# RWKV scan: the eight diagonal blocks of a lane in one transfer from evenly spaced DRAM rows, 8 loads a chunk in place of 16

## The reference, cut to what matters

```python
def step(S, inp):
    r_t, w_t, k_t, v_t, kk_t, b_t = inp
    sa = jnp.einsum('bhij,bhj->bhi', S, -kk_t)
    S = (S * w_t[:, :, None, :] + sa[..., None] * b_t[:, :, None, :]
         + v_t[..., None] * k_t[:, :, None, :])
    return S, jnp.einsum('bhij,bhj->bhi', S, r_t)
```

## Time and profile before

| | us |
|---|---|
| Median of 3 runs | 3494.68 |
| Lowest and highest of them | 3493.44, 3499.32 |
| The profiled execution | 3487.46 |
| Its span, first to last instruction | 3486.2 |

### The profile page before, as it was taken

How to read it: one execution, slowest core, us unless ns; L and a number is a source line. 1 busy time by engine, 2 the same in 40 slices (tenths; PEclk the granted TensorE clock), 3 DMA queues, 4 the chain that set the end, 5 groups by cost and what they waited for, 6 DMA issues and landing times.

```text
span 3486.2 us, 58522 instructions
## 1 busy us (share of the span) xinstructions
PE 3188.2 (91%) x25755; PEld 2622.4 (75%) x25755; DVE 2211.3 (63%) x2948; ACT 971.9 (28%) x1514; POOL 469.5 (13%) x373
## 2 busy tenths in 40 slices
PE   6988788979987999999999897998998799999996
PEld 4777767778885878888888676875667688888885
DVE  5758655778887444444444575997556566666666
ACT  4544233312113221111111444112663111111112
POOL 2530023423224000000000121000001011111110
PEclk9979788989998999999999998999999899999999
DMA  4410044322224011111111202114001111111111
GB/s 131 122 66 14 16 142 138 111 45 42 37 36 166 19 55 51 40 55 53 38 55 43 91 31 74 49 43 99 2 2 61 43 49 49 49 49 49 49 49 67
DMA packets 242726, 207.27 MB, mean 59 GB/s; under 512 B 66744, under 2 KB 205255, under 8 KB 241959
## 3 DMA queue, kind: packets, MB, share of 16 engines
q1 hardware_dynamic: 223527, 176.82, 17.1%
q10 hardware_dynamic: 13824, 25.17, 2.2%
q0 software_dynamic: 5120, 1.53, 0.5%
HBM read 171.93 MB, written 29.64 MB: 58 GB/s over the span
## 4 chain that ended last, share of the span: by engine, by line
PE 70%; DVE 17%; ACT 5%; POOL 2%; issue 2%; DMA 2%; SPq 1%; ACTq 0%; DVEq 0%; POOLq 0%
PE ps L2169 23%; PE ps L2184 17%; PE ps L2031 5%; PE ps L636 3%; PE ps L637 3%; PE ps L638 3%; DVE Yc L2794 2%; DVE s_tmp L1662 2%; DVE s_Z L1663 2%; PE ps L2893 2%; PE ps L2921 1%; PE ps L2911 1%; PE ps L1480 1%; POOL a_x L2544 1%; PE ps L1008 1%
## 5 line engine op out<-in xcount | busy, mean ns | idle before, releaser
L3198 DVE TENSOR_TENSOR H<-H,ps 128x1024 f32<-128x1024 f32 x256 | 312.7, 1221 | 181.6 <-PE ps L2184 174.8
L2334 DVE TENSOR_TENSOR fsum<-fsum,ps 128x1024 f32<-128x1024 f32 x168 | 205.2, 1221 | 312.4 <-PE ps L2184 310.3
L2184 PE MATMUL ps<-dh,hh 128*128 128x512 f32 x864 | 340.0, 393 | 19.9 <-DVE hl L2149 13.9
L2184 PE MATMUL ps<-dl,hh 128*128 128x512 f32 x864 | 338.7, 392 | 0.0
L2184 PE MATMUL ps<-dh,hl 128*128 128x512 f32 x864 | 338.6, 392 | 0.0
L2169 PE MATMUL ps<-hn_h,uh 128*128 128x512 f32 x704 | 275.8, 392 | 7.2 <-DVE ul L1779 4.7
L2169 PE MATMUL ps<-hn_l,uh 128*128 128x512 f32 x704 | 275.4, 391 | 0.0
L2169 PE MATMUL ps<-hn_h,ul 128*128 128x512 f32 x704 | 275.3, 391 | 0.0
L2169 PE MATMUL ps<-hx_h,uh 128*128 128x512 f32 x512 | 200.9, 392 | 8.4 <-DVE hx_l L2149 5.3
L2184 PEld LDWEIGHTS ps<-dh,hh 128*128 128x128 f32 x864 | 163.8, 190 | 58.0 <-DVE hl L2149 15.6
L2169 PE MATMUL ps<-hx_l,uh 128*128 128x512 f32 x512 | 200.4, 391 | 0.0
(11 more groups left out here) (473 smaller groups left out, 7345.8 us busy)
## 6 DMA issues: line engine op xcount, KB each, us to landing
aw<-in_w_ada_dram ACTq DMA_DIRECT2D x96, 256.0 KB, 2.9
uw<-in_w_mlp_dram SPq DMA_DIRECT2D x32, 512.0 KB, 4.3
dw<-in_w_mlp_dram SPq DMA_DIRECT2D x32, 512.0 KB, 5.2
uw<-in_ffn_gate_dram SPq DMA_DIRECT2D x22, 512.0 KB, 4.0
uw<-in_ffn_up_dram SPq DMA_DIRECT2D x22, 512.0 KB, 5.3
dw<-in_ffn_down_dram SPq DMA_DIRECT2D x22, 512.0 KB, 5.9
cw<-in_w_in_dram SPq DMA_DIRECT2D x20, 512.0 KB, 3.8
o_w<-in_w_out_dram SPq DMA_DIRECT2D x16, 512.0 KB, 9.9
```

The lines of the kernel that those rows point to most:

```text
L2184: mm = pe.e.matmul(ps[:, 2 * pair + hf, :], v[s][:, blk(t)], w[:, half(hf)], start=(m == 0), stop=(m == 2))
L2334: return dve.c.tensor_tensor(f, f, new, ALU.add) if g else dve.c.tensor_copy(f, new)
L3198: return dve.c.tensor_tensor(h, h, self.ps[:, 4 + 2 * (t % 2):6 + 2 * (t % 2), :], ALU.add)
```

## The change

The scratch `nd` gets another shape: for each lane two halves (one for each head of the pair) of 64x64 elements and 64 elements of padding. With the padding, going from one diagonal block to the next is always 16 rows and 16 columns, 1,040 elements, also from the last block of the first half to the first block of the second. So one load can take the 8 blocks of a lane: 8 by 16 rows by 64 bytes. There are 8 loads, of 8 KB each, SP has 4 of them (x = 0 and 1), POOL the other 4.

Three things follow. The store of `NM` is made in two DMAs, one for each half of the partitions, both ahead of the `ZZ` loads in SP's queue. The order of the partitions of `N16` and `Z16` becomes x, k in place of k, x. And the store of `Z16` to `zd`, whose DRAM order stays k, x, so writes its 32 rows of 4 KB as 4 groups (x) of 8 (k), the rows of a group 16 KB apart; it was one contiguous run.

```diff
-                         ("nd", (2, LANES, PART, CH)), ...
+                         ("nd", (2, LANES, 2, CH * CH + CH)), ...
-    def blocks_there(self, eng, counter, n, ks):
-        nd = self.dram["nd"]
-        for k in ks:
+    def blocks_there(self, eng, counter, n, xs):
+        nd = self.dram["nd"][n % 2]
+        for x in xs:
             for d in range(2):
-                eng.e.dma_start(self.N16[4 * k:4 * k + 4, d], nd[n % 2, 4 * d:4 * d + 4, 16 * k:16 * k + 16, 16 * (k % 4):16 * (k % 4) + 16]) \
+                eng.e.dma_start(self.N16[8 * x:8 * x + 8, d], bass.AP(tensor=nd.tensor, offset=nd[4 * d + x].offset, ap=[[16 * CH + 16, 8], [CH, 16], [1, 16]])) \
                     .then_inc(*counter.one("in", n))
...
-            sp.e.dma_start(nd[n % 2].rearrange("l p c -> p l c"), self.NM[n % 3][:, :, 0, :]).then_inc(*self.t_n.one("out", n))
+            for H in range(2):
+                sp.e.dma_start(nd[n % 2, :, H, 0:CH * CH].rearrange("l (p c) -> p l c", c=CH), self.NM[n % 3][H01[H], :, 0, :]).then_inc(*self.t_n.one("out", n))
...
-            self.blocks_there(sp, self.t_n, n, range(0, 5))
+            self.blocks_there(sp, self.t_n, n, range(0, 2))
...
-            sp.e.dma_start(zd[n % 2].rearrange("k x d w i c -> (k x) (d w i c)"), self.Z16[:].rearrange("p d w i c -> p (d w i c)")) \
+            sp.e.dma_start(zd[n % 2].rearrange("k x d w i c -> x k (d w i c)"), self.Z16[:].rearrange("p d w i c -> p (d w i c)")) \
                 .then_inc(*self.t_z.one("out", n))
...
-                self.blocks_there(pool, self.t_nb, n, range(5, 8))
+                self.blocks_there(pool, self.t_nb, n, range(2, 4))
```

More of the change, by code:

```diff
@@ L232, in __init__ @@
         for n, shape in (("h", (NBLK, PART, D)), ("rows", (4, D)), ("la", (NBLK, PART, 512)), ("sg", (2, NBLK + 1, PART, RW)), ("lo", (3, PART, TOK)),
-                         ("nd", (2, LANES, PART, CH)), ("zd", (2, 8, 4, 2, 2, 16, 16)), ("v", (PART, 4, TOK)), ("y_gla", (PART, 4, TOK)),
+                         ("nd", (2, LANES, 2, CH * CH + CH)), ("zd", (2, 8, 4, 2, 2, 16, 16)), ("v", (PART, 4, TOK)), ("y_gla", (PART, 4, TOK)),
                          ("rpb", (HEADS, RPB_R, GRID, PART))):
```

## The result

| | before | after |
|---|---|---|
| Median us | 3494.59 (20 runs) | 3509.95 (20 runs) |
| Lowest to highest | 3487.98 to 3502.74 | 3499.3 to 3519.0 |
| The profiled execution | 3487.46 | 3511.23 |

The ratio is 1.0042, with a 95% interval of 1.0033 to 1.0052: slower by 15.4 us between the medians, where 8.1 were forecast. The measured 3510 us lie inside the stated range of 3496 to 3515, but above the forecast's own range, which ended at +11.1.

A forecast was written before the change was run, and what follows sets the result against it. It took TensorE to bound the kernel, but nm, SP's queue to `ZZ` and DVE each chunk's path. Terms 7.0 + 0.9 + 1.0 - 0.8 made +8.1 us, about 3503 us; own range +5.1 to +11.1, stated 3496 to 3515.

The forecast's parts named there:

- The `N16` loads are hidden: In the scan, products and doubling cover these loads, so halving them gains nothing in 15 chunks.
- The first chunk: DVE's 3.67 us wait for `N16` there: 1.24 us gained, less 0.48 for the second `nd` store, -0.8 us.
- The second `nd` store: In SP's queue between nm and the `ZZ` loads: SP's four start 0.48 us later, POOL's do not.
- The `zd` store: Ahead of both queues' `ZZ` loads: written in 4 groups it runs on 4 engines, not 16, landing 0.9 us later.
- any delay of `zd` counts at once: At SP's `ZZ` loads: SP's `nd` store ends about when `zd` lands, so a later `zd` delays them directly.
- The handovers: `ZZ` to TensorE, 16 chunks: ten at 0.7 us make 7.0, the last +0.9, the other five 1.0.
- The five chunks' cover of 0.5: Where TensorE arrives later than `ZZ`: 0.5 us of the delay is hidden, 0.2 remain, five times makes 1.0 us.
- Rival 1: The `zd` store is slower still, +1.7 us, so SP's `ZZ` loads wait too: +20.9 us, 3516 us; chance 0.10.
- Rival 2: The `zd` store costs what it did; only SP's `ZZ` loads move, by 0.48: +2.8 us, 3497.5 us; chance 0.22.
- Rival 3: `ZZ` loads get a freer road, giving back up to 0.9 us a chunk: -6, about 3488 us; chance 0.08.

The follow-up runs named there:

- e3: Kernel before with only the `zd` store changed, to 4 groups by padding after every 8 rows; 3508.64 us, ratio 1.0041.
- e2: Kernel before with only the `nd` store cut into two halves of 64 partitions, both ahead of the `ZZ` loads; 3502.26 us, ratio 1.0029.
- e5: Changed kernel with loads into every fourth partition of `N16`, so the order stays k, x and the `zd` store is contiguous; 3496.90 us, ratio 1.0003.
- e1: Changed kernel with only the `zd` store made contiguous again, so the inverted blocks go back in the wrong order; 3500.05 us, ratio 1.0010.
- e10: Changed kernel with its two `nd` stores issued by ACT instead of SP, `zd` store left in 4 groups; 3508.91 us, ratio 1.0036.
- e4: Kernel before with only the `zd` store changed, to 8 groups by padding after every 4 rows; 3492.50 us, ratio 0.9993.
- e9: Kernel before with only the `zd` store changed, to 2 groups by padding after every 16 rows; 3544.77 us, ratio 1.0137.

## Why the prediction came out as it did, step by step

- **The `N16` loads are hidden: right in direction, incomplete.** The changed kernel waits for them once, 3.8 us, as before. But they have a worth where something else is late. In e3, with the `zd` store in groups and sixteen loads, DVE waits for `N16` 6 times, 8.9 us:

```profile
DVE s_tmp L1662 <- DMA s_N<-nd_dram: 8.9, 6, 3.4
```

  In the changed kernel, with eight, once. And e2 (sixteen loads, two stores) is 0.26% above e5 (eight loads, two stores), with intervals that just do not touch; e1, the same comparison without the stride, is 0.19% below e2 with intervals that do. The waits for `N16` are 4.4 us in e2 against 1.5 in e5, which covers a third. The clock fell in six chunks of the profiled e2, in four of e5 and in two of e1, which may be the rest; this is not shown.
- **The first chunk: -0.8 forecast, neither borne out nor refuted.** In the changed kernel's profile POOL's four loads take 2.56 us there instead of 3.86, but they start 0.75 us later behind the two stores, and DVE waits as long, 3.8 us. The profile shows a landing of up to 3.6 us among them, against a median of 2.3. In e1, whose first chunk has the same loads and stores up to there, DVE waits 1.3 us. So the one profiled execution does not settle this term.
- **The second `nd` store: mis-sized, and then covered.** Forecast 0.48, measured 0.88 (e2); SP issues a store from 64 partitions in 634 ns and one from 128 in 381. In the changed kernel this does not matter (e10). The prediction had SP's start at the later of the two conditions and so had the cover right; e2 alone shows that the price as such was too low.
- **The `zd` store: the mechanism was right, and its size was too small.** This is the term that the experiments tie to the loss: e1 takes it out, e3 puts it alone into the kernel before. Forecast +0.9, measured 3.37 - 1.91 = +1.46. The prediction had two bounds, +0.9 from the pace of the `sig` load and +1.7 from the store's own pace with 16 engines, and took the lower one. The truth lies between: six more pieces at 0.24 us each, not 0.187 and not 0.29. The sentence that any delay of `zd` counts at once is wrong for SP: e4 has 0.39 us of it and loses nothing. The sum itself had this cover (0.5 for SP, 0.9 for POOL). By the Trainium skill's rule on the number of engines (DMA: Bandwidth & Descriptors, "Why a DMA increments its semaphore by 16 and not by 1") the stores of e3, e4 and e9 run on 4, 8 and 2 engines. Their landings agree with it; no row counts the engines.
- **The handovers.** With `zd` 0.9 late the shift was to be 0.7 in ten chunks. With 1.46 both sets start 1.06 to 1.46 later, the middle is 1.26; in the prediction's own sum, with nothing for the first chunk, 12.6 + 1.5 + 5 x 0.8 = 18.1 us. Measured were 15.4 between the medians, and in the profiled execution 22, of which I estimate 15 at the full clock. Two terms of opposite sign are missing from the sum: the `ZZ` loads land faster (next point), and the clock falls in chunks where TensorE has waited. So that 18.1 comes near the measured time does not confirm each term. The five chunks' cover of 0.5 was not measured apart.
- **The rivals.** Rival 1 (+20.9) was nearer than the forecast in the landing (3.6 forecast, 3.4 measured) and in the time too, 5.5 us off against 7.3. Rival 2 fell with the landing. Rival 3, a freer road for `ZZ`, shows in part, though it did not decide. The median landing of a `ZZ` load falls from 2.7 us to 2.3, and SP issues its four in 2.08 us (median over the chunks) instead of 2.43, though in some chunks, as in the timeline above, it still takes 2.93. e3, with sixteen `N16` loads and the same late `zd`, has 2.3 as well. So it goes with the later start behind the `nd` store and not with the fewer loads behind.
- **The range.** The forecast's own range, +5.1 to +11.1, does not hold the 15.4. The stated one does because it was stretched to just short of rival 1. That the result falls inside is in part luck.

## What to carry to other kernels

When an edit reorders the partitions of a tile, look at the transfers on the tile's other side: here the loads that were halved were hidden behind other work, and the one store that took on the new order lay on the path. A store with few rows in its slowest dimension landed later here, 3.31 us with 4 against 1.91 with 32; a dummy change of that dimension alone (padding, as in e3, e4, e9) prices it. And two waits that end at nearly the same time do not add: undo each alone, in the new kernel and in the old, before a loss is shared out. And read the granted clock of the stretch before and after: a longer wait of TensorE can come with slower matmuls behind it, which no sum of waits has in it.

## What the runs showed of the hardware

- The landing of a store of 32 rows of 4 KB: 1.91 us with 32 rows in the slowest dimension of its destination, 2.30 with 8, 3.31 with 4, 4.88 with 2. With 8 the kernel's time shows no difference (e4, 0.9993).
- SP's time to issue a DMA depends on its shape by a factor of two: 381 ns for a store from 128 partitions and 634 for one from 64; 318 for the contiguous `zd` store and 591 to 647 for the grouped ones of e3, e4 and e9; 323 for a load into 8 neighbouring partitions and 682 into every fourth.
- The granted clock of TensorE was 1.00 from 740 to 1060 us in the kernel before, with 13.9 us of waits for `ZZ` in the scan. In the changed kernel, with 29.6 us of them, it was 0.50 in parts of five chunks. Over the scan of e9, with 48.6 us of them, it was 0.93. In the changed kernel a chunk that begins with the lower clock takes 24.7 us, the others 23.4.
